# PE multiplies a constant matrix at four places where it waits for its next input

## What is computed

```python
def reference(x, ...):
    x = first_block(x, ...)            # ends: return rms_norm(h, final_norm)
    return second_block(x, ...)

def second_block(x, c, ...):
    h = x * (1.0 + sc1) + sh1
    z = h @ w_in[l] + b_in[l]
    ...
    x = layer_norm(DEEPNORM_ALPHA * x + g1 * mix, ln1_g[l], ln1_b[l])
    h = x * (1.0 + sc2) + sh2
    f = jnp.square(jax.nn.relu(h @ w_m1[l] + b_m1[l])) @ w_m2[l] + b_m2[l]
    x = layer_norm(DEEPNORM_ALPHA * x + g2 * f, ln2_g[l], ln2_b[l])
```

## Time and profile before

| | us |
|---|---|
| median of 3 runs | 2534.09 |
| lowest and highest | 2532.17, 2542.75 |
| the profiled execution | 2535.02 |
| its span, first to last instruction | 2533.20 |
| PE busy in the span | 2467.1 (97%) |
| DVE busy | 1708.3 (67%) |
| ACT busy | 1032.3 (41%) |
| mean granted clock of PE | 0.991 |

### The profile page before, as it was taken

How to read it: one execution, slowest core, us unless ns; L and a number is a source line. 1 busy time by engine, 2 the same in 40 slices (tenths; PEclk the granted TensorE clock), 3 DMA queues, 4 the chain that set the end, 5 groups by cost and what they waited for, 6 DMA issues and landing times.

```text
span 2533.2 us, 31225 instructions
## 1 busy us (share of the span) xinstructions
PE 2467.1 (97%) x13558; PEld 2101.8 (83%) x13558; DVE 1708.3 (67%) x1613; ACT 1032.3 (41%) x942; POOL 21.0 (1%) x44
## 2 busy tenths in 40 slices
PE   7999999999999999989999999999899999999998
PEld 7988888787778888778888888898788888888886
DVE  7766567776677777766676786657775655555555
ACT  4543454334334334354544342133443343443442
POOL 0000000000000000000000000000000000000000
PEclk9999999999999999999999999999999999999999
DMA  6333466676776887855666774245555555555552
GB/s 256 135 117 133 166 211 260 265 289 252 291 286 255 313 305 288 308 216 214 233 259 256 270 274 170 100 183 183 199 183 187 195 184 195 187 185 198 183 195 105
DMA packets 78634, 549.94 MB, mean 217 GB/s; under 512 B 8763, under 2 KB 10966, under 8 KB 12833
## 3 DMA queue, kind: packets, MB, share of 16 engines
q1 hardware_dynamic: 74832, 528.25, 56.3%
q0 software_dynamic: 3664, 19.69, 2.0%
HBM read 541.61 MB, written 6.29 MB: 216 GB/s over the span
## 4 chain that ended last, share of the span: by engine, by line
PE 85%; DVE 8%; ACT 3%; DMA 2%; issue 1%; SPq 0%; ACTq 0%; DVEq 0%
PE ps L530 25%; PE ps L531 13%; PE ps L543 11%; PE ps L545 10%; PE ps L544 10%; DVE w_lo L1349 3%; DMA stage<-wstream 2%; ACT w_hi L969 2%; PE ps L528 2%; PE ps L498 1%; PE ps L499 1%; PE ps L500 1%; PE ps L918 1%; PE ps L906 1%; PE ps L816 1%
## 5 line engine op out<-in xcount | busy, mean ns | idle before, releaser
L1349 DVE TENSOR_TENSOR w_lo<-stage,w_hi 128x2048 fp32r<-128x2048 f32 x402 | 918.1, 2288 | 533.1 <-ACT w_hi L969 530.5
L969 ACT ACTIVATE w_hi<-stage 128x2048 fp32r<-128x2048 f32 x402 | 766.3, 1910 | 859.1 <-DMA stage<-wstream 396.7
L530 PE MATMUL ps<-xs,w_hi 128*128 128x512 f32 x3000 | 1063.6, 398 | 3.5 <-DVE w_lo L1349 2.5
L531 PE MATMUL ps<-xs,w_lo 128*128 128x256 f32 x3000 | 842.9, 281 | 0.0
L530 PEld LDWEIGHTS ps<-xs,w_hi 128*128 128x128 f32 x3000 | 563.5, 188 | 140.4 <-DVE w_lo L1349 5.2
L531 PEld LDWEIGHTS ps<-xs,w_lo 128*128 128x128 f32 x3000 | 567.5, 189 | 4.1 <-issue 0.2
L543 PE MATMUL ps<-w_hi,hs 128*128 128x512 f32 x1024 | 402.3, 393 | 9.9 <-DVE w_lo L1349 9.9
L544 PE MATMUL ps<-w_hi,hs 128*128 128x512 f32 x1024 | 400.0, 391 | 0.0
L545 PE MATMUL ps<-w_lo,hs 128*128 128x512 f32 x1024 | 399.8, 390 | 0.0
L543 PEld LDWEIGHTS ps<-w_hi,hs 128*128 128x128 f32 x1024 | 192.9, 188 | 54.6 <-DVE w_lo L1349 12.7
L544 PEld LDWEIGHTS ps<-w_hi,hs 128*128 128x128 f32 x1024 | 193.1, 189 | 40.6 <-issue 0.7
(11 more groups left out here) (372 smaller groups left out, 2430.4 us busy)
## 6 DMA issues: line engine op xcount, KB each, us to landing
stage<-wstream SPq DMA_DIRECT2D x497, 1024.0 KB, 4.9
spectra<-k_made POOLq DMA_DIRECT2D x4, 1024.0 KB, 4.2
k_spec<-spectra POOLq DMA_DIRECT2D x4, 1024.0 KB, 6.7
xraw<-xT SPq DMA_DIRECT2D x4, 512.0 KB, 11.1
resid<-x SPq DMA_DIRECT2D x2, 1024.0 KB, 15.2
out<-out_t SPq DMA_DIRECT2D x4, 512.0 KB, 2.6
c_row<-c_row POOLq DMA_DIRECT2D x1, 1024.0 KB, 5.1
w<-w POOLq DMA_DIRECT2D x8, 128.0 KB, 4.3
```

The lines of the kernel that those rows point to most:

```text
L530: pe.matmul(o2, hi, rhs[:, k, :], start=(first and j == 0), stop=False)
L531: mm = pe.matmul(o2[:, S:2 * S], lo, rhs[:, k, 0:S], start=False, stop=False)
L969: act.activation(w_hi[:, w % HIGH, 0:m], stage[:, n % RING, 0:m], ACT.Copy).then_inc(hi_ready, 1)
L1349: tt(w_lo[:, slot, 0:m], stage[:, slot, 0:m], f(w_hi[:, w % HIGH, 0:m]), ALU.subtract).then_inc(lo_ready, 1)
```

## The change

A helper on PE issues n matmuls of `ones` by `ones` (128x128 by 128 columns, float32) into the first 128 columns of a PSUM bank, each with start and stop set, so that nothing is added up and nothing is read. It is called with bank 7 at the four places, ahead of the wait that stands there: 70 calls at the start (behind a new wait for `ones_ready`), 40 before seam f, 58 before seam ln1, 58 before the tail. That is 226 calls. No other instruction changes.

```diff
+        def keep_running(n, bank):
+
+            for _ in range(n):
+                pe.matmul(ps[:, bank, 0:P], ones[:], ones[:], start=True, stop=True)
+
+        pe.wait_ge(sem("ones_ready"), 1)
+        keep_running(70, 7)
         for w in range(T_IN, T_QB):
             tile(w, xin, (lambda g: (sem("xin_ready"), g + 1)) if w < T_IN + 2 else None)
...
+        keep_running(40, 7)
         for n in range(3):
             turn_normed("f", n)
...
             tile(w, mixs, (lambda g: (evac_done, U_BB + 2 * (g + 1))) if w < T_WO + 4 else None)
+        keep_running(58, 7)
         for n in range(3):
             turn_normed("ln1", n)
         mlp(T_MLP2, U_MLP2, lambda g: (sem("ln1_lo"), g + 1), hook=lambda: turn_normed("ln1", 3))
+        keep_running(58, 7)
         pe.wait_ge(evac_done, U_END)
```

## The result

The changed kernel takes 2541.14 us, the kernel before 2536.23, both medians of 16 runs; the ratio is 1.0021, with a 95% interval from 1.0014 to 1.0029. That is slower by 5 us, inside the half per cent that the prediction counts as "no change", and less than half of the 11.8 us forecast. The time lies in the range of 2540 to 2551, near its lower end.

A forecast was written before the change was run, and what follows sets the result against it. The prediction took PE, busy 97% of the span, to bound the kernel. Costs of 0.5 (start), 2.8 (f), 4.8 (ln1) and 3.7 (tail) summed to 11.8 us, giving 2545.9 us on the median's scale; range 2540 to 2551.

The forecast's parts named there:

- a call is two records: Each dummy matmul makes two PE records, 0.1116 us apiece, 0.223 us a call at full clock.
- ln1: At seam ln1 the dummies outlast the gap, so the first transposed block and the tile behind it come 4.8 us later.
- The tail: At the tail the dummies outlast the gap and delay the last blocks and stores; cost taken as 3.7 us.
- The start: At the start real PE work begins at 19.0 us, not 13.06, but this costs only 0.5 us (0.0 to 0.7).
- the first rival: Start stays at low clock longer: rise after 6.9 us takes the sum past 12.7 us, no rise +15.1; chance 0.10.
- seam f: At seam f the dummies outlast the gap, so the first block and the tile behind it come 2.8 us later.
- the granted clock should stay 1.00 through both seams: At seams f and ln1 PE's clock would no longer fall from its full 2.4 GHz.
- Nothing catches it up: Behind seam f, ACT, DVE and PE's first tile all follow the late block, so the 2.8 us stays lost.
- can't gain: At the start the warm clock buys time on PE where DVE is the bound; cost 0.5 us, no gain.
- Eaten downstream: Rival: delays shrink where PE later waits for something it doesn't set; without f's 2.8 us, 2543.1 us; chance 0.06.
- The dummies fit: Rival: one record a call, dummies end before the waits at seams and tail; -3.9 us, 2530.2 us; chance 0.06.
- Transposes at the low level behind dummies: Rival: at seams and tail transposes run at low clock even after dummies; 16.7 us in all, 2550.8 us; chance 0.02.

The follow-up runs named there:

- run 12: Changed kernel with 64 calls at the start instead of 70, the other three places as changed: 2548.63 us, 1.0051 of the kernel before.
- run 2: Changed kernel without the start's wait and 70 calls, keeping 40, 58 and 58 at the seams and tail: 2547.61 us, 1.0046 of the kernel before.
- run 4: Changed kernel with only the 58 calls at the tail kept: 2540.29 us, 1.0014 of the kernel before.
- run 1: Changed kernel with only the 70 calls at the start kept: 2528.21 us, 0.9967 of the kernel before.
- Run 11: Kernel before plus 30 calls ahead of PE's weight tile 20, near 174 us, none elsewhere: 2528.24 us, 0.9971 of the kernel before.
- run 3: Changed kernel with no start calls and 22, 31 and 31 calls at the seams and tail: 2534.88 us, 0.9994 of the kernel before.
- run 5: Changed kernel with 30 calls at the start instead of 70, none at the seams and tail: 2529.78 us, 0.9973 of the kernel before.
- start64: Changed kernel with 64 calls at the start instead of 70, none at the seams and tail: 2535.63 us, 0.9999 of the kernel before.

## Why the prediction was right and where it was wrong

**Right: a call is two records.** 452 records, 116 of them in 13.11 us. Everything about the three later places rests on it.

**Right in the time, in part by luck.** 2541.14 is a cost that was forecast well and a gain of 6.4 us that was forecast as nothing. That the two together stay above 2540 is luck: 1.2 us more of the gain and the time would lie outside the range.

**Right: the sum of the costs.** With the code-place effect taken away (run 12), the whole change costs 12 to 13 us, forecast 11.8; the seams and the tail alone cost 11.7, forecast 11.3. One by one: ln1 4.8 forecast, 4.81 measured in the changed kernel and in run 2. The tail 3.7 forecast, 4.2 in the changed kernel, 4.1 in the trace of run 4 and 3.5 by its median: the last block was evacuated at 2534.78, 17.8 us after the first dummy as forecast, and the stores ended 4.3 us behind it, not 3.9. The start 0.5 forecast, +1.04 at r_x in the changed kernel and +0.30 in run 1; r_x scatters from -0.21 to +0.66 in runs 2 to 4, whose start is unchanged, so the term is not tested to better than about 1 us. PE's first record of real work came 0.49 us later than forecast; from 18.5 us for 140 records, at 0.216 or 0.112 each, the rise lay 6.0 us behind the first dummy, outside the assumed 4.0 to 5.5 but short of the 6.9 from which the first rival would have held.

**Mis-sized: seam f.** 2.8 forecast to the first tile, 2.81 in run 2 and in the changed kernel, which then lost another 0.68. The step that failed there is "the granted clock should stay 1.00 through both seams": after 1.84 us of idle time it fell to 0.50 at 1116.3. The argument for 1.00 was one row at 46.81, with an idle time of 2.31 us and no fall of pace. One such row shows that a fall is not certain, not that it won't come; ln1 and run 2 had the same 1.84 us without a fall. Run 11, whose code is that of before until 172 us, even shows the fall at the very place of that row: its tile at 47.36 comes after 2.32 us of idle time, and the granted clock is 0.57 from 47 to 51. Both falls came after shorter gaps than the one that the prediction quotes; what was measured decides.

**Wrong: everything outside the four places was taken as fixed.** The prediction says "Nothing catches it up" of seam f and "I know of no fixed event", and of the start that it "can't gain". It treated added instructions as work in time only. They are also length of code, and behind them every instruction of PE sits at another place in its 256-instruction block. Where a block is fetched, a load that is under way can land late, and a tuned kernel whose weight loads land just in time answers to that, with -6.4 us here. None of the rivals had this mechanism. "Eaten downstream" came nearest in size, but it lost f's delay behind f; the gain lies ahead of f. It could have been suspected from the profile's page, which lists the q8 packets, and from the w_lo waits of 6.7 us in the stretch; it could not have been sized, not even its sign, without a run.

**The rivals.** "The dummies fit" is refuted as an account of this change. As an idea it gave -1.5 in run 3, not the -3.9 it was priced at, with an interval from -3.6 to +0.8: it gave the tail 2 us, which got 0.8, and ln1 0.94, of which the clock left 0.28. "Transposes at the low level behind dummies" is refuted: 24 of them ran in 2.78 us. The Trainium skill ("TensorE: Matmul & The Clock Gate", Part 4: PE-mode transpose) says that the full clock doesn't engage for transposes; behind matmuls that had raised it, it held for all 24 here. "The start stays low for longer" did not reach its 6.9 us with 128 columns (6.0) and came in full with one.

## What to carry to other kernels

Price a warm-up matmul from a row of the same type and shape, records per call first, and let the count end before the wait does: here 40 and 58 calls cost 12 us where 22 and 31 gained 1.5, if anything. Before crediting a small change in an engine's code with a gain or a loss, pad the code by a whole fetch block and by a fraction of one: if 64 calls do nothing and 6 calls do everything, the calls are not the reason. Then look at which loads are under way when the instruction packets come. In a stretch that DMA feeds just in time such padding was worth more here than the change itself, but it had to be found by trial and may be lost with the next edit.

## What the runs showed of the hardware that was not expected

- The place of PE's code against its 256-instruction blocks moved the whole kernel by 6 to 8 us (0.9967 to 0.9976 with 24 or 120 instructions more, 0.9999 with 256), through the waits for weight tiles 700 us further on. Loads of 1 MB that were under way at an instruction packet took 7.4 to 9.0 us behind the two waits followed above, others 6.8 to 7.1.
- A plain f32 matmul with one column takes as long as one with 128 at the low clock (0.21 us a record), and the pace stayed low through all 140 of them (30.03 us). In the traces that start with 128-column ones it rose 3.0 (start64) to 6.0 us (the changed kernel) behind the first.
- In run 5 the dummies stop 3.12 us before the real work, and it begins at the low pace.
- The clock fell at three of ten seams that look alike, each with 1.80 to 1.85 us of idle time behind transposes at the full clock.
- The clock column says 1.00 for the first 10 us (run 5) while the first records come at the low pace: there only the distance between records tells.
